# Router on raw rows with folded weights: norms, row stores and turns of the early tiles inside the attention

## The reference

```
rmsnorm(x)  = x * rsqrt(mean(x*x) + 1e-6) * g
h           = rmsnorm(x) * (1 + scale) + shift            # modulate
logits      = h @ w_router                                # tokens x 16 experts
affinity    = softmax over the 16 experts
gates, idx  = top_k(affinity, 2*n/16)                     # each expert picks its tokens
y_e         = (silu(h[idx] @ w_gate) * (h[idx] @ w_up)) @ w_down * gates
x           = x + gate * scatter_add(y_e)
```

## Time and profile before

| | |
|---|---|
| median of 3 runs | 2344.65 us (2342.02 to 2346.42) |
| profiled execution | 2346.8 us, span 2345.0 us |
| PE busy | 2085.9 us (89%) |
| PEld, DVE, ACT, POOL busy | 982.1, 823.6, 501.5, 93.8 us |
| DMA | 504.69 MB, mean 215 GB/s |
| mean granted TensorE clock | 0.965 |
| expert weights | 3 x 128 loads of 1024 KB |

### The profile page before, as it was taken

One profiled execution on the slowest core, in us unless ns is written; L12 is line 12 of the kernel. 1 busy time (PEld: TensorE's weight loads), 2 busy tenths in 40 slices (PEclk: granted clock), 3 DMA queues, 4 the chain that ended last, 5 costly groups with the idle time before them and its releaser, 6 DMA issues.

```text
span 2345.0 us, 27739 instructions
## 1 busy us (share of the span) xinstructions
PE 2085.9 (89%) x10964; PEld 982.1 (42%) x10964; DVE 823.6 (35%) x2114; ACT 501.5 (21%) x1173; POOL 93.8 (4%) x69
## 2 busy tenths in 40 slices
PE   5998989999975999999999799999997589898886
PEld 3434455556542333333333456456554233333332
DVE  3321355767744021120211532376765301010102
ACT  3210153545420010010100321165443000000000
POOL 1100100000001000000000110000000000000000
PEclk9999999999987999999999899999999799999999
DMA  9865020000045988989889202020002899999995
GB/s 335 311 237 215 1 73 1 1 1 1 1 173 209 399 340 351 366 320 400 337 327 369 84 19 72 7 66 1 1 1 101 338 420 419 420 419 420 420 420 216
DMA packets 89611, 504.69 MB, mean 215 GB/s; under 512 B 10162, under 2 KB 15196, under 8 KB 35852
## 3 DMA queue, kind: packets, MB, share of 16 engines
q1 hardware_dynamic: 84832, 487.00, 52.5%
q0 software_dynamic: 2880, 10.49, 1.3%
q10 hardware_dynamic: 1772, 5.43, 0.6%
HBM read 495.55 MB, written 7.34 MB: 214 GB/s over the span
## 4 chain that ended last, share of the span: by engine, by line
issue 71%; PE 18%; DMA 7%; DVE 3%; POOL 1%; ACT 0%; POOLq 0%; DVEq 0%; ACTq 0%
PE psS L523 11%; PE psT L523 4%; DMA arena<-in_w_down 2%; DMA arena<-in_w_gate 2%; DMA arena<-in_w_up 2%; PE psO L523 1%; PE psM L523 1%; DVE idx L1604 1%; DVE arena L1603 0%; DMA arena<-normed_rows,LIU 0%; PE psO L526 0%; DVE arena L1606 0%; ACT arena L938 0%; PE psM L526 0%; PE psS L526 0%
## 5 line engine op out<-in xcount | busy, mean ns | idle before, releaser
L523 PE MATMUL psS<-arena 128*64 128x512 f32 (+7 forms) x4832 | 1207.7, 559 | 65.7 <-DMA arena<-in_w_up 28.6
L523 PEld LDWEIGHTS psS<-arena 128*64 128x64 f32 (+3 forms) x4832 | 473.8, 157 | 696.1 <-issue 646.5
L526 PE MATMUL psT<-ident,arena 128*128 128x128 f32 (+1 forms) x936 | 152.3, 295 | 92.3 <-DVE arena L1514 29.8
L1657 DVE TENSOR_TENSOR arena<-arena,psS 128x512 f32<-128x512 f32 x32 | 20.6, 684 | 503.3 <-PE psS L523 503.3
L526 PEld LDWEIGHTS psT<-ident,arena 128*128 128x128 f32 (+1 forms) x936 | 111.0, 150 | 172.9 <-issue 91.6
L938 ACT ACTIVATE arena<-psS 128x128 f32<-128x128 f32 (+5 forms) x138 | 50.7, 400 | 602.5 <-PE psS L523 568.6
L523 PE MATMUL psM<-arena 128*128 128x512 f32 x384 | 171.9, 595 | 4.0 <-DVE X L1460 3.0
L1500 DVE TENSOR_REDUCE mx<-psS 128x1 f32<-128x768 f32 (+2 forms) x200 | 165.0, 825 | 29.1 <-PE psS L523 27.6
L523 PE MATMUL psT<-arena 128*32 128x512 f32 x1536 | 174.7, 595 | 0.0
L938 ACT ACTIVATE arena<-psS,nb 128x768 f32<-128x768 f32 (+2 forms) x200 | 158.9, 795 | 71.0 <-DVE nb L1505 69.4
L523 PE MATMUL psO<-arena 128*64 128x128 f32 (+2 forms) x1632 | 167.9, 304 | 3.3 <-ACT arena L938 1.8
(11 more groups left out here) (184 smaller groups left out, 1218.8 us busy)
## 6 DMA issues: line engine op xcount, KB each, us to landing
arena<-in_w_gate SPq DMA_DIRECT2D x128, 1024.0 KB, 15.9
arena<-in_w_up SPq DMA_DIRECT2D x128, 1024.0 KB, 12.5
arena<-in_w_down SPq DMA_DIRECT2D x128, 1024.0 KB, 17.8
arena<-in_w_mod SPq DMA_DIRECT2D x34, 1024.0 KB, 7.2
gtb<-in_w_mod SPq DMA_DIRECT2D x14, 1024.0 KB, 6.6
arena<-in_w_in SPq DMA_DIRECT2D x6, 2048.0 KB, 8.9
normed_rows<-arena ACTq DMA_DIRECT2D x10, 512.0 KB, 15.5
arena<-in_w_out SPq DMA_DIRECT2D x8, 512.0 KB, 7.9
```

Source lines behind the costliest of these rows:

```text
L523: return nc.tensor.matmul(o, lhsT, rhs, start=start, stop=stop)
L526: return nc.tensor.transpose(o, in_, ident[0:n, 0:n])
L1657: last = V.tensor_tensor(ar[:, a:a + 512], ar[:, a:a + 512], bank(2 * g + h), ALU.mult)
```

## The change

The router no longer reads modulated rows. Its weights are multiplied by the modulation's gain (`router_weights`, DVE, at slot 2 of the layer's first tile), the shift's share of the logits is made there once as `rb` by 16 (layer 0) or 8 (layer 1) small matmuls (`router_bias`, PE), and the logits are `raw row @ folded weights`, scaled by the row's root `rn` and added to `rb`. They come out by token: 8 matmuls a tile with 128 columns of stationary X turned and 16 moving columns. The normed rows are still stored for the gather.

Roots move to slots 12 and 14 of the next tile (one tile at a time), the scaled row and its store to ACT at slot 16, the turns of raw X of the early tiles (all but the last) to the steps after the last slot (`TAIL`). The softmax and affinity turns are done once for all early tiles and once for the last tile. The last tile's second O goes to bank 6 and doesn't wait for the first half's residual. PE adds to `open` after the last tile's logits instead of after its O. The gates for the expert output come last. A semaphore of its own (`s_xl`) counts the last tile's store.

```diff
@@ pool
-                powers(len(TILES[l]) + 1)
+                powers(2 * len(TILES[l]))
-                pool.wait_ge(s_xd, 16 * (l * TT + len(TILES[l])))
+                pool.wait_ge(s_xd, 16 * (l * (TT - 1) + len(TILES[l]) - 1))
+                pool.wait_ge(s_xl, 16 * (l + 1))
@@ tensor
+                def router_bias():
+                    for k in range(2 if l == 0 else 1):
+                        for x in range(KD):
+                            m, w = l * 96 + 48 + k * 8 + x, l * P + x * NE
+                            last = mm(bank(5, col=k * NE, w=NE), view(modcol, 0, P, m, (0, P)), wrt[:, w:w + NE], x == 0, x == KD - 1)
+                def turn_rows(n, h):
+                    c = 2 * n + h
+                    if c >= 3:
+                        pe.wait_ge(z["xt"], c - 2)
+                    if n == n_tiles - 1:
+                        pe.wait_ge(z["me"], end + 1 + h)
+                    for x in range(4):
+                        last = tr(bank(c % 3, col=x * P, w=P), view(X, ...))
+                def logits(n, h):
+                    pe.wait_ge(z["xt"], 2 * n + h + 1)
+                    for k in range(4 * h, 4 * h + 4):
+                        last = mm(bank(3, col=t * NE, w=NE), ar[:, a:a + P], w, k == 0, k == KD - 1)
...
                         elif s == 2:
                             pe.wait_ge(z["gtev"], 4 * l + 4)
+                            router_bias()
...
+                job("T", n_tiles - 1, 0)
...
+                logits(n_tiles - 2, 0)
+                logits(n_tiles - 2, 1)
+                job("O", n_tiles - 1, 0)
+                pe.wait_ge(z["prb"], 2 * l + 1)
+                affinities(tl[:-1])
+                job("O", n_tiles - 1, 1)
+                turn_rows(n_tiles - 1, 0)
+                logits(n_tiles - 1, 0)
+                turn_rows(n_tiles - 1, 1)
+                logits(n_tiles - 1, 1)
                 pe.sem_inc(z["open"], 1)
-                gates(5, "fht", (0, 1, 2, 3))
-                (turns of XN2, 512-column router matmuls, turns of logits and affinities)
+                pe.wait_ge(z["prb"], 2 * l + 2)
+                affinities(tl[-1:])
+                gates(5, "fg", (0, 1, 2, 3))
@@ scalar
+                def store_rows(i):
+                    act.wait_ge(z["fxn"], l * TT + i + 1)
+                    a_(ar[:, a:a + D], X[:, t * D:(t + 1) * D], ACT.Identity, scale=rn[:, t:t + 1]).then_inc(z["xr"], 1)
+                    act.wait_ge(z["xr"], l * TT + i + 1)
+                    act.dma_start(rows[t * P:(t + 1) * P, :], ar[:, a:a + D])
...
+                        if slot == 16 and i:
+                            store_rows(i - 1)
@@ vector
+                    if s == 2:
+                        router_weights()
+                    if s is not None and s >= SLOTS and s % SLOTS == 12:
+                        root_begin(s // SLOTS - 1)
+                    if s is not None and s >= SLOTS and s % SLOTS == 14:
+                        root_end(s // SLOTS - 1)
```

More of the change, by code:

```diff
@@ L125, in attention_plan, with tail_steps @@
         plan.append((s if s < n else None, v, mult, jobs, ready.get(s + 1)))
-    last = len(tiles) - 1
-    plan.append((None, None, None, [("T", last, 0), ("O", last, 0), ("O", last, 1)], None))
-    return plan
+    return plan
+def tail_steps(plan, early):
+    steps = [n for n, entry in enumerate(plan) if entry[0] is None][1:]
+    return {step: n for n, step in enumerate(steps[:early])}
 def uses_act(sec, t):
@@ L188, in jobs_through @@
     n = len(Q_PLACE)
-    for _, _, _, jobs, _ in plan:
+    last = max(i for _, _, _, jobs, _ in plan for _, i, _ in jobs)
+    for _, _, _, jobs, _ in plan + [(None, None, None, [("T", last, 0), ("O", last, 0), ("O", last, 1)], None)]:
         for j in jobs:
@@ L294, in backbone_program @@
         TMP = 36608
+        LG4, WRC = 0, TT * NE
+        XT, XROW = QT, WOUT + 7 * D
         LAMP = TMP
@@ L608, in job @@
                     first = kind == "Q" and i == 0
-                    b = (7, 6, 5, 7)[r] if first else 7
-                    if not first or r == 3:
+                    final = kind == "O" and i == len(tiles) - 1 and r
+                    b = (7, 6, 5, 7)[r] if first else 6 if final else 7
+                    if (not first or r == 3) and not final:
                         pe.wait_ge(z["me"], mj)
@@ L819, in _, with affinities @@
-                last.then_inc(z["at"], 1)
+                    if step in TAIL:
+                        n = TAIL[step]
+                        turn_rows(n, 0)
+                        turn_rows(n, 1)
+                        if n:
+                            logits(n - 1, 0)
+                            logits(n - 1, 1)
+                F = FP[l]
+                tl = TILES[l]
+                def affinities(ts):
+                    for t in ts:
+                        o = bank(4, 0, NE, (t - TC) * P, P) if t >= TC else bank(5, 0, NE, t * P, P)
+                        last = tr(o, scm[:, LG4 + t * NE:LG4 + (t + 1) * NE])
+                    last.then_inc(z["at"], 1)
@@ new lines, in _ @@
+                job("T", n_tiles - 1, 0)
+                for n in range(len(TAIL), n_tiles - 1):
+                    turn_rows(n, 0)
+                    turn_rows(n, 1)
+                    if n:
+                        logits(n - 1, 0)
+                        logits(n - 1, 1)
+                logits(n_tiles - 2, 0)
[4 more added lines that the diff above has]
+                job("O", n_tiles - 1, 1)
@@ new lines, in affinities @@
+                def affinities(n):
+                    ts = tl[:-1] if n == 0 else tl[-1:]
+                    dve.wait_ge(z["at"], 2 * l + n + 1)
+                    c0, c1 = max(ts[0] - TC, 0) * P, (ts[-1] - TC + 1) * P
+                    last = V.tensor_copy(ar[0:NE, AFF + c0:AFF + c1], bank(4, 0, NE, c0, c1 - c0))
+                    if l == 0 and n == 0:
+                        last = V.tensor_copy(ar[32:48, AFF:AFF + CTX], bank(5, 0, NE, 0, CTX))
+                    link(last)
+                probabilities(0)
@@ L1601, in _ @@
+                n = len(tl) - 1
+                dve.wait_ge(z["xp"], 2 * n + 2)
+                a = XT + n % 4 * D + 512
+                V.tensor_copy(ar[:, a:a + 512], bank((2 * n + 1) % 3)).then_inc(z["xt"], 1)
+                root_begin(n)
+                root_end(n)
+                probabilities(1)
+                affinities(1)
                 for r in range(CAP_L // 8):
```

221 lines of the change are left out of this document (107 added, 114 removed).

## The result

The changed kernel takes 2355.18 us (median of 9 runs, 2350.6 to 2359.42); the kernel before, on the same chip, 2346.61 (2342.02 to 2350.77). The ratio is 1.0036, 95% interval 1.0022 to 1.0050: slower by 8.6 us. The forecast was 2343.0, with a range from 2335 to 2349.

A forecast was written before the change was run, and what follows sets the result against it. PE was taken to bound layer 0's experts, the weight stream layer 1's. Terms 3.9 + 1.2 + 1.75 - 7.3 - 1.2 = -1.65 us took profiled 2346.8 to 2345.1; the median lies 2.15 lower: 2343.0, range 2335 to 2349.

The forecast's parts named there:

- part 1: Tail up to top-k: ring opens 14.5 and 8.0 us later, top-k starts 8.9 and 7.7 sooner in layers 0 and 1.
- two halves of 7.0: Layer 0's tail: the last tile's O takes two halves of 7.0 us, starting at 672.3 and ending at 687.0.
- Part 3, the roots: DVE's root instructions at slots 12 and 14, 0.8 us a tile, mostly covered; with row stores 1.75 us in all.
- Part 3, ACT's row store: Scaling and store at slot 16 take ACT 1.6 us, mostly covered by idle time; with roots 1.75 us in all.
- The rival that put it on the path: ACT's row store delays slot 17's exponent and PE, 12.8 us instead of 1.75: 2354.0 us; chance 0.12.
- Part 3, the bias: `router_bias` behind slot 2's scores in the first tile costs 3.9 us in layer 0 and 1.2 in layer 1.
- Part 2, the gather: Gathers share DMA engines with the later weight loads: 7.3 of 8.9 us left in layer 0, 1.2 gained in layer 1.
- The sign named for part 2: Layer 1's second gather landing in over 9 us shows the gather part right, under 7 wrong.
- The first rival: Gather hardly slowed, ring nearly full: layer 1 keeps 5.2 to 6.4 us instead of 1.2, 2339.0 to 2337.8; chance 0.22.
- narrow matmuls pipe: Bias and logit calls at 0.13 us each save 9.4 us more, all on the path: 2333.6 us; chance 0.08.
- the fourth rival: Tail runs by hops, not PE: each half tile waits 0.9 us for its copy before logits: 2351.5 us; chance 0.06.
- the second and third: Rivals: narrow matmuls pipe (2333.6 us, chance 0.08) and ACT's row store on the path (2354.0 us, chance 0.12).

The follow-up runs named there:

- c2: The changed kernel with each logit matmul moving 128 columns instead of 16, computing the same; 2349.43 us, ratio 1.0003 to the kernel before.
- b0_after_again: The changed kernel itself measured once more, nothing altered; 2356.96 us, ratio 1.0038 to the kernel before.
- a4: The changed kernel, but SP issues nine weight loads and the tenth only when the first gathers have landed; 2345.17 us, ratio 0.9993.
- d1: c4 and c3 in one: folded bias, wide logits, early tiles' roots on GpSimd, first five ring slots opened early; 2329.40 us, ratio 0.9924.
- c4: b3 without SP's wait for the gathers; the first five ring slots open before the last early tile's logits instead; 2334.87 us, ratio 0.9954.
- c3: b2 with the early tiles' roots worked out by GpSimd instead of DVE; 2333.83 us, ratio 0.9948.
- a3: The changed kernel with logit matmuls moving 128 columns instead of 16, from wrong columns, so tokens are routed otherwise; 2349.82 us, ratio 1.0009.
- b2: b1 and the gather wait of a4 in one; 2341.75 us, ratio 0.9977.
- b3: b2, but GpSimd sums the bias products, leaving PE one bias matmul a stream instead of eight, same result; 2339.0 us, ratio 0.9969.
- d4: d1 with the ring opening whole and late again, as in the changed kernel; 2340.01 us, ratio 0.9968.
- b1: The changed kernel with every bias and logit matmul moving 128 columns instead of 16, computing the same; 2345.71 us, ratio 0.9992.

## Why the prediction was wrong

**No term for the granted clock: the step that failed first.** The sum priced 16-column matmuls by their call time, and that was right: 0.23 against 0.22 forecast. With wide logits (c2), behind which the clock stays up, part 1 came out and a little more: top-k is 10.0 and 8.8 us sooner (8.9 and 7.7 forecast), and the first O of layer 0 is 12.2 later (12.6). But "two halves of 7.0" holds in no trace with narrow logits: the clock falls at or before the first. With the shortest falls, in `b0_after_again` and a4, top-k is 8.5 and 7.1 sooner; in the first profile it is 3.8 and 5.5. Put back into d1 the narrow logits cost 6.1 us. The prediction never asked what a run of narrow matmuls does to the clock, and kept the prices of O in the earlier trace rows, which were taken at full clock, behind a run that did not stand there. The Trainium skill, "TensorE: Matmul & The Clock Gate", Part 1, says that the clock's two levels follow how busy PE has been recently. By the profile's busy time that does not tell these cases apart: PE was busy for all of 672 to 684 in the changed kernel, and the clock fell; with 128 moving columns in the same calls it did not.

**Part 3, the roots: mis-sized, by reading a row at the wrong place.** I took 1.75 us for roots and stores, with the argument that DVE idles 1.01 us for PE "right there". That wait, at 512.09, is slot 17's. The roots stand at slots 12 and 14, where DVE idles 0.22 and 0.43 us, and in the last tile of a layer the four instructions cost 1.0 us whole. The steps of the lag sum to 4.7, of which 3.8 stay; by ratios it is 7.0. Of the rest, 1.5 can be seen in layer 0's tail, whose first O comes 18.6 us after the last turn in all four traces that have wide logits and the roots on GpSimd, and 20.1 to 20.2 in the six with wide logits and the roots on DVE. That is the granted clock again. In the six it is at 0.50 for 3.4 us right behind the last turn, and the 24 products with the values there take longer, first c4, then d1:

```profile
656.09 2.83 PE L549 MATMUL psO<-arena 128*64 128x128 f32 x24
```

```profile
655.59 1.53 PE L569 MATMUL psO<-arena 128*64 128x128 f32 x24
```

The stretch isn't bound to where the roots are made: layer 1 of c3, with the roots on GpSimd, has it (first O at 14.6), layer 1 of a3 and c2, with the roots on DVE, has not (13.1). So part of the 7.0 may be where the clock happens to fall; what the four instructions themselves cost is shown as 3.8.

**Part 3, ACT's row store: right.** The scaling takes 1.15 us and the issue 0.33 at slot 16, and in no latent tile does the lag rise behind them. In the context tile it rises by 0.2 to 0.3 up to slot 19, in every changed kernel; 0.7 was forecast for that tile, roots included. The rival that put it on the path is refuted; that its time of 2354.0 is close to the measured one is luck.

**Part 3, the bias: about right in size, not in its make-up.** Forecast 3.9 and 1.2, together 5.1. Where the clock stayed up the wide bias made the lag grow by 4.5 and 2.0, at the upper bounds of 4.4 and 2. Of that the calls are 3.2 and 1.7 us (wide against folded), and 1.3 and 0.4 stay even with one call. The narrow bias put back into d1 costs 3.8 by ratios and 2.6 by medians, which is not clear of noise; with the 1.7 that d1 still has that is 5.5. The first profile's 8.8 and 2.8 contain a low clock which came between slots 2 and 12 in 13 of the 17 traces of changed kernels: in all six with the narrow bias, in two of five with the wide one, in five of six with one call a stream, and not in the one trace of the kernel before. Up to there b2 and c3 are alike, and so are b3 and c4; in each pair one trace has the stretch and the other has not. So in layer 0 the narrow bias isn't shown to be its cause. Narrow bias traces have more of it (mean growth 8.5 against 3.7 with one call), but medians don't bear out a difference that large.

**Part 2, the gather: right in kind, too small.** Forecast was that the sooner top-k loses 1.6 us in layer 0 and 6.5 in layer 1 to the loads. From gather to PE's turns layer 0 went from 8.5 to 12.6 (11.3 in b0), a loss of 2.8 to 4.1; layer 1 from 6.7 to 12.9, 6.2. d4 shows 3.6 and 5.8, and 10.3 in the ratios. So layer 1 was sized rightly and layer 0 not. There I had the ring open at 39.9 after the last turn and the gather done 10.1 us after its issue. The later opening, 40.9 to 45.9, is not what made the difference: in a3, b1 and c2 the ring opens at 39.3 to 39.5, and PE turns the rows 11.4 to 11.5 us after the issue. The sign named for part 2 came: the second gather of layer 1 landed in 11.5 us. The first rival (gather hardly slowed) is refuted, and with it what the Trainium skill's "DMA: Bandwidth & Descriptors" on packet-by-packet alternation was taken to give, a loss of only 2.5 us in layer 1.

**Together.** Forecast: bias 5.1, roots 1.75, gather 8.1, top-k -16.6, sum -1.65. Measured: bias 5.5, roots 3.8 (by the lag) to 7.0 (by ratios), gather 9.4 (by traces), clock 6.1, top-k -18.8 (with wide logits, c2), and 1.5 back at the end of layer 1 (494.6 us from the experts' start to the end became 493.1). That is 4.5 to 7.7, against 8.6 and 9.5 in the two series; three of the terms are known to 4 us only, so 1 to 5 us are left open. The largest misses are the clock, put at nothing and measured at 6.1, and the roots, put at no more than 1.75 and measured at 3.8 to 7.0.

Of the other rivals, that narrow matmuls pipe at 0.13 a call is refuted (0.23), and the tail did run by PE, not by hops.

Two slips in the prediction change no reading. The growth that it names for layer 0's attention, 5.7, is 5.2 by its own terms; measured were 9.1 and, in layer 1, 4.5 against 1.7. And the range left out the fourth rival (2351.5) as well as the second and third, so 0.26 lay outside it and not 0.20.

## What to carry to other kernels

Price a new kind of matmul twice: its own calls, and what the granted clock does to the work behind it. Where only few columns are needed, moving 128 of them and letting the rest fall on columns that are overwritten cost 5% more time in the calls here and saved 6 to 8 us. Low stretches come and go between two profiles of one kernel, so a variant is judged by several of its traces and by its ratio, not by one profile. Cover must be looked up at the very slot at which an instruction is put: a saturated engine's idle time two slots later is no cover. And when a stage is pulled forward, look at what the transfers that open next to it will be doing: here a gather that came sooner met a ring that opened later, and opening part of the ring over dead buffers cured both.

## What the runs showed of the hardware

- 16 f32 records with 16 moving columns take 1.86 us, with 128 columns 1.95, at the same 128 stationary columns and full clock.
- The granted clock fell from 1.00 to 0.50 with PE busy without a gap, in all seven traces with narrow logits, in both layers, and in none of the ten with wide ones at that place. Behind the bias of layer 1 it fell in all six traces with the narrow one and in none of the other eleven. The same program showed the fall in layer 0's tail some 6 us earlier or later (14.3 against 20.7 us after the last turn), so that two profiles of one kernel differ by up to 5 us in one tail and by 3 in the first tile. What else makes it fall in the first tile of layer 0 stays open.
- A gather of indexed rows that took 6.8 us from issue to PE's turns with the ring of weights full (d1, layer 1) took 12.7 inside the stream that fills it (d4).
